# A gated-delta block: from the second block on, diagonal blocks of 32 are inverted on VectorE and one stage is left to TensorE

## The reference

```python
lower = jnp.where(strict, beta[..., :, None] * kk * decay, 0.0)
eye = jnp.eye(CHUNK, dtype=jnp.float32)
rhs = jnp.concatenate([beta[..., None] * v, beta[..., None] * k * jnp.exp(gc)[..., None]], axis=-1)
a_mat = jnp.broadcast_to(eye, lower.shape) + lower
sol = lax.linalg.triangular_solve(a_mat, rhs, left_side=True, lower=True, unit_diagonal=True)
```

## Time and profile before

| what | value |
|---|---|
| median of three executions | 2792.9 us (2784.8 to 2797.9) |
| the profiled execution | 2790.5 us |
| its span, first to last instruction | 2788.7 us |
| TensorE busy | 2710.8 us, 97% |
| VectorE busy | 1507.9 us, 54% |
| GpSimd busy | 1652.9 us, 59% |
| ScalarE busy | 1057.0 us, 38% |

### The profile page before, as it was taken

One profiled execution on the slowest core, in us unless ns is written; L12 is line 12 of the kernel. 1 busy time (PEld: TensorE's weight loads), 2 busy tenths in 40 slices (PEclk: granted clock), 3 DMA queues, 4 the chain that ended last, 5 costly groups with the idle time before them and its releaser, 6 DMA issues.

```text
span 2788.7 us, 36083 instructions
## 1 busy us (share of the span) xinstructions
PE 2710.8 (97%) x13344; PEld 2265.9 (81%) x13344; DVE 1507.9 (54%) x2439; ACT 1057.0 (38%) x1831; POOL 1652.9 (59%) x1244
## 2 busy tenths in 40 slices
PE   5999999999999999999999999999999999999998
PEld 4778887888888888888888888888888888888886
DVE  5878666474748566654546456563544553322223
ACT  3533332353334424343334433343333333433332
POOL 3745453676556756575556756575555666665653
PEclk9999998999999999999999999999999999999999
DMA  7334334432333323322233323422222223222232
GB/s 276 119 121 144 121 140 137 146 129 95 110 110 129 106 75 122 129 86 89 81 122 101 112 77 102 147 87 87 88 87 84 87 87 136 98 98 95 95 129 83
DMA packets 98094, 311.56 MB, mean 112 GB/s; under 512 B 11520, under 2 KB 11520, under 8 KB 95872
## 3 DMA queue, kind: packets, MB, share of 16 engines
q1 hardware_dynamic: 67248, 246.85, 25.5%
q10 hardware_dynamic: 30672, 62.40, 6.7%
HBM read 285.09 MB, written 24.12 MB: 111 GB/s over the span
## 4 chain that ended last, share of the span: by engine, by line
PE 86%; DVE 8%; issue 2%; POOL 2%; DMA 1%; ACT 1%; ACTq 0%; SPq 0%; POOLq 0%; DVEq 0%
PE acc L506 24%; PE acc L508 24%; PE acc L507 24%; PE pm L541 6%; PE pm L546 2%; DVE mixing L1229 1%; POOL w L1678 1%; PE pm L667 1%; PE pm L637 1%; DMA mixing<-in_ada_w 1%; PE pm L642 1%; DVE x L1510 1%; DVE octs L1334 1%; PE pm L638 1%; PE pm L653 0%
## 5 line engine op out<-in xcount | busy, mean ns | idle before, releaser
L1678 POOL TENSOR_TENSOR w<-raw,w 128x512 fp32r<-128x512 f32 x832 | 1134.1, 1366 | 1000.3 <-ACT w L749 998.0
L749 ACT ACTIVATE w<-raw 128x512 fp32r<-128x512 f32 x832 | 520.6, 627 | 775.9 <-PE acc L508 723.3
L506 PE MATMUL acc<-mT,w 128*128 128x512 f32 x1536 | 623.8, 406 | 8.5 <-DVE mT L1572 3.2
L508 PE MATMUL acc<-mT,w 128*128 128x512 f32 x1536 | 602.9, 393 | 0.0
L507 PE MATMUL acc<-mT,w 128*128 128x512 f32 x1536 | 601.5, 392 | 0.0
L506 PE MATMUL acc<-hid,w 128*128 128x512 f32 x864 | 348.8, 404 | 4.3 <-DVE ffs L1470 3.5
L506 PEld LDWEIGHTS acc<-mT,w 128*128 128x128 f32 x1536 | 291.4, 190 | 67.9 <-issue 5.1
L508 PEld LDWEIGHTS acc<-mT,w 128*128 128x128 f32 x1536 | 290.3, 189 | 63.4
L508 PE MATMUL acc<-hid,w 128*128 128x512 f32 x864 | 337.4, 390 | 0.0
L507 PE MATMUL acc<-hid,w 128*128 128x512 f32 x864 | 336.8, 390 | 0.0
L507 PEld LDWEIGHTS acc<-mT,w 128*128 128x128 f32 x1536 | 291.6, 190 | 54.8 <-issue 1.0
(11 more groups left out here) (231 smaller groups left out, 3697.4 us busy)
## 6 DMA issues: line engine op xcount, KB each, us to landing
raw<-in_w_all SPq DMA_DIRECT2D x416, 512.0 KB, 3.5
ada_late<-in_ada_w SPq DMA_DIRECT2D x32, 512.0 KB, 5.1
xr<-in_xT ACTq DMA_DIRECT2D x48, 256.0 KB, 3.5
mixing<-in_ada_w SPq DMA_DIRECT2D x8, 1024.0 KB, 9.8
proj_kept<-ffs ACTq DMA_DIRECT2D x32, 256.0 KB, 2.1
out<-io ACTq DMA_DIRECT2D x32, 256.0 KB, 2.4
mixed_kept<-mixing ACTq DMA_DIRECT2D x28, 256.0 KB, 2.2
xr<-mixed_kept ACTq DMA_DIRECT2D x28, 256.0 KB, 2.7
```

The lines of the kernel that those rows point to most:

```text
L506: e.matmul(bank, whi, x[:, 0, :], start=first, stop=False)
L508: m = e.matmul(bank, wlo, x[:, 0, :], start=False, stop=last)
L749: e.activation(w2[:, 0, local % HALVES, :], raw[:, tile % NRAW, local % 2 * NT:(local % 2 + 1) * NT], ACT.Copy).then_inc(S["w_hi"], 1)
L1678: e.tensor_tensor(w2[:, 1, local % HALVES, :], raw[:, tile % NRAW, local % 2 * NT:(local % 2 + 1) * NT], w2[:, 0, local % HALVES, :].bitca ...
```

## The change

From unit 4 on (`wide(n)`), VectorE inverts diagonal blocks of 32 rather than 8, in 31 steps of multiply, shuffle and add, two steps in each of the slots 19 to 34; TensorE's stage 0 and what belongs to it on the other engines is left out, and stage 1 keeps its slots. The mask of `Lm` moves from VectorE to GpSimd for all units. `attn` moves from slot 18 to 27, the two SiLUs from 21 to 26 and 28, `states` and `orr` one slot later, and the gates for the next block three slots later. Semaphore counts follow. One more mask of 128x128 is loaded at the start, and unit 4 makes two small constants.

```diff
@@ -590,8 +635,8 @@
-                if s in (16, 19, 23, 27):
-                    t = (16, 19, 23, 27).index(s)
+                if s in (16, 20, 24, 28):
+                    t = (s - 16) // 4
...
-                if 0 <= st < STAGES and step == 0:
-                    e.wait_ge(S["lvl_mask"], STAGES * n + st + 1)
-                    if st == 0:
+                if first_stage(n) <= st < STAGES and step == 0:
+                    e.wait_ge(S["lvl_mask"], stage_at(n, st) + 1)
+                    if st == first_stage(n):
...
                     e.wait_ge(S["proj_evac"], UNIT * m + RK + 1)
                     e.wait_ge(S["rot_q"], m)
                     e.wait_ge(S["r_upd"], m)
+                    if m and wide(m - 1):
+                        e.wait_ge(S["oct_steps"], oct_done(m))
...
+                if s == 18 and wide(n):
...
+                    e.wait_ge(S["oct_masked"], n + 1)
+                    e.tensor_reduce(wide_cols(near32), by_wide(Lm).rearrange("p t b j -> p t j b"), AX.X, ALU.add).then_inc(
+                        S["oct_steps"], 1)
+                    e.wait_ge(S["eye32_ready"], 2)
+                    e.wait_ge(S["r_upd"], n + 1)
+                    e.wait_ge(S["oct_steps"], oct_done(n) + 1)
+                    e.stream_shuffle(row32[0], near32, [0] * WIDE).then_inc(S["oct_steps"], 1)
+                for i in (range(2 * (s - 19), min(2 * (s - 19) + 2, WIDE - 1)) if wide(n) and 19 <= s < 35 else ()):
+                    done, low = oct_done(n) + 2 + 3 * i, i + 1 if i else 0
+                    row = wide_cols(row32[i % 2])
+                    before = wide_cols(inv32) if i else eye32.unsqueeze(1).to_broadcast([P, SUB, WIDE])
+                    e.wait_ge(S["oct_steps"], done)
+                    e.tensor_tensor(wide_cols(part32)[:, :, low:], row[:, :, low:],
+                                    before[:, :, i:i + 1].to_broadcast([P, SUB, WIDE - low]), ALU.mult).then_inc(S["oct_steps"], 1)
+                    if i + 1 < WIDE - 1:
+                        e.stream_shuffle(row32[(i + 1) % 2], near32, [i + 1] * WIDE).then_inc(S["oct_steps"], 1)
+                    e.wait_ge(S["oct_steps"], done + 1)
+                    e.tensor_tensor(wide_cols(inv32)[:, :, low:], before[:, :, low:], wide_cols(part32)[:, :, low:],
+                                    ALU.add).then_inc(S["oct_steps"], 1)
+                if s == 35 and wide(n):
+                    e.wait_ge(S["oct_steps"], oct_done(n + 1))
...
+                if s == 27:
+                    e.tensor_tensor(attn, bF, Dm, ALU.mult).then_inc(S["attn_ready"], 1)
...
+                if s == 17:
+                    e.wait_ge(S["lt_ready"], n + 1)
+                    near_mask = lmask32[:, :] if wide(n) else lmask[:, 0, :]
+                    e.tensor_tensor(by_sub(Lm), by_sub(LT), over_subs(near_mask), ALU.mult).then_inc(S["oct_masked"], 1)
+                if s in ((34,) if wide(n) else (26, 34)):
```

More of the change, by code:

```diff
@@ L36, with wide, oct_done, first_stage @@
 OCT = 8
+WIDE = 32
 OSTEPS = 1 + 3 * (OCT - 1)
+WSTEPS = 1 + 3 * (WIDE - 1)
+def wide(n):
+    return n >= HEADS
+def oct_done(n):
+    return OSTEPS * min(n, HEADS) + WSTEPS * max(n - HEADS, 0)
+def first_stage(n):
+    return 1 if wide(n) else 0
+def stage_count(n):
+    return STAGES * min(n, HEADS) + (STAGES - 1) * max(n - HEADS, 0)
+def stage_at(n, st):
+    return stage_count(n) + st - first_stage(n)
 SLOTS = 64
@@ L70, in dense_plan @@
                 e = kept[4 * n:4 * n + 4]
-                new = p[0:2] + e[0:1] + p[2:5] + e[1:2] + p[5:6] + e[2:3] + p[6:7] + e[3:4] + p[7:8]
+                if n:
+                    new = p[0:2] + e[0:1] + p[2:5] + e[1:2] + p[5:6] + e[2:3] + p[6:7] + e[3:4] + p[7:8]
+                else:
+                    new = p[0:4] + e[0:1] + p[4:6] + e[1:2] + p[6:7] + e[2:3] + p[7:8] + e[3:4]
             else:
@@ L342, in near_row, with wide_cols, by_wide @@
             return oct_cols(3 + i)
+        def wide_cols(ap):
+            return ap.rearrange("p (t j) -> p t j", j=WIDE)
+        near32, inv32 = (octs[:, 4 * i:4 * i + 4, :].rearrange("p a c -> p (a c)") for i in range(2))
+        row32 = [swp[:, i * P:(i + 1) * P] for i in range(2)]
+        part32 = swp[:, 2 * P:3 * P]
+        eye32 = octs[:, 8, :]
+        same32 = small[:, 48:52]
+        def by_wide(ap):
+            return ap.rearrange("p (t b j) -> p t b j", t=SUB, j=WIDE)
         def by_oct(ap):
@@ L608, in mix @@
                     else:
-                        e.wait_ge(S["t_next"], (STAGES - 1) * n + st)
+                        e.wait_ge(S["t_next"], n + 1)
                     four(bE, Lm, T).then_inc(S["x_out"], 1)
[L611 to L614, removed]
+                if first_stage(n) <= st < STAGES and step == 2:
+                    e.wait_ge(S["x_ready"], stage_at(n, st) + 1)
+                    if st > first_stage(n):
+                        e.wait_ge(S["u_turned"], n + 1)
                     else:
@@ L1321, in mix @@
                                            in1=sub(bA, t), op0=ALU.mult, op1=ALU.add).then_inc(S["r_state"], 1)
-                if s == 18:
-                    e.tensor_tensor(attn, bF, Dm, ALU.mult).then_inc(S["attn_ready"], 1)
-                    e.wait_ge(S["oct_steps"], OSTEPS * n + 1)
+                if s == 17:
+                    e.wait_ge(S["kk_out"], n + 1)
+                    e.wait_ge(S["beta_d"], n + 1)
+                    e.tensor_tensor(LT, bB, bD, ALU.mult).then_inc(S["lt_ready"], 1)
+                if s == 19 and not wide(n):
+                    e.wait_ge(S["oct_masked"], n + 1)
+                    e.tensor_reduce(near, by_oct(Lm).rearrange("p t b j -> p t j b"), AX.X, ALU.add).then_inc(S["oct_steps"], 1)
+                    e.wait_ge(S["oct_steps"], oct_done(n) + 1)
                     for i in range(OCT - 1):
-                        e.stream_shuffle(octs[:, 3 + i, :], octs[:, 0, :], [OCT * (q // OCT) + i for q in range(32)]).then_inc(S["oct_steps"], 1)
-                if 19 <= s < 19 + OCT - 1:
-                    i = s - 19
-                    done = OSTEPS * n + OCT + 2 * i
+                        e.stream_shuffle(octs[:, 3 + i, :], octs[:, 0, :], [OCT * (q // OCT) + i for q in range(32)]).then_inc(
+                            S["oct_steps"], 1)
+                for i in {20: (0, 1), 21: (2, 3), 22: (4, 5), 23: (6,)}.get(s, ()) if not wide(n) else ():
+                    done = oct_done(n) + OCT + 2 * i
                     if n == 0 and i == 0:
@@ L1337, in mix @@
                     e.tensor_tensor(inv8, before, part8, ALU.add).then_inc(S["oct_steps"], 1)
-                if s == 26:
-                    e.wait_ge(S["oct_steps"], OSTEPS * (n + 1))
+                if s == 25 and not wide(n):
+                    e.wait_ge(S["oct_steps"], oct_done(n + 1))
                     e.tensor_tensor(by_oct(U), inv8.unsqueeze(2).to_broadcast([P, SUB, P // OCT, OCT]),
```

135 lines of the change are left out of this document (71 added, 64 removed).

## The result

The changed kernel takes 2861.6 us, the median of four executions (2861.2 to 2871.6), beside 2790.6 for the kernel before: a ratio of 1.0268, 95% interval 1.0244 to 1.0292. It is 2.7% slower. The forecast was 2846 with a range of 2767 to 2900 and 0.68 for slower.

A forecast was written before the change was run, and what follows sets the result against it. TensorE, busy 97% of the span, was taken to bound the kernel. From the profiled 2790.5 us, 38.9 us of dropped calls were subtracted and 94 us of standing for VectorE added: 2846 us, range 2767 to 2900.

The forecast's parts named there:

- The gain: TensorE drops 48 stage-0 calls in 12 units at 0.81 us each, 38.9 us, counted in full.
- The step: One multiply, shuffle and add on VectorE takes 0.60 us undisturbed; 31 steps take 18.6 us a unit.
- The hold: GpSimd operations hold VectorE's multiplies and adds: 0.8 us for each of 198 in the windows, 158 us.
- VectorE's need: VectorE needs 414 + 158 = 572 us in the twelve windows, which TensorE would pass in 448.
- Standing and clock: TensorE stands 124 - 30 = 94 us in the windows for late VectorE; the sum had no clock term.
- The room: VectorE may be late by 2.5 us a unit, 30 us in all, before TensorE stands.
- The place: New idle time before dense matmuls, released by VectorE's evictions, slots 19 to 35, most in units 5 and 6, least in 11.
- TensorE's busy time: Sign of being right: in the new profile TensorE is busy about 39 us less.
- The moved slots: Moving orr, the SiLUs, attn and gates to other slots costs nothing; 12 us if dense products don't cover them.
- VectorE hides it: Rival, chance 0.12: GpSimd operations and steps seldom meet in the windows, TensorE never stands, 2751.6 us.
- GpSimd gives way: Rival, chance 0.20: GpSimd waits in dense VectorE runs, 0.5 us a meeting gives 2787 us, 0.4 gives 2767.
- Lateness drags the others: Rival, chance 0.16: ScalarE and GpSimd fall behind with VectorE, as if each hold cost 1.05 us, 2895 us.

The follow-up runs named there:

- kernel 2: Changed kernel with 7 of the 31 steps in a wide unit, one a slot, inverse left incomplete: 2757.3 us, ratio 0.9875 to the kernel before.
- kernel 3: Changed kernel with each multiply and add of the 31 steps replaced by a shuffle of the same size, inverse not computed: 2786.4 us, ratio 0.9976.
- Kernel 9: kernel 2 plus 14 reductions of 128x512 on VectorE ahead of slot 30's addition of squares in units 4, 8 and 12: 2791.3 us, ratio 0.9999.
- Kernel 4: Changed kernel with 16 of the 31 steps, one in each of slots 19 to 34, inverse left incomplete: 2787.6 us, ratio 0.9989.
- Kernel 5: Changed kernel with the MLP norm's column sums and what follows them two slots later in units 4, 8 and 12: 2861.4 us, ratio 1.0247.
- kernel 1: Changed kernel with no wide unit, only the moved slots and the mask of Lm on GpSimd left: 2792.9 us, ratio 1.0000.
- kernel 8: Changed kernel, all twelve units wide, multiply and add fused into one instruction per part, narrower shuffle, MLP norm two slots later: 2932.3 us, ratio 1.0501.

## Why the prediction was right

The direction, the mechanism and nearly the size were right: 2861.3 us in the profiled execution against 2845.6. Step by step:

- **The gain.** Forecast 38.9 us; kernel 2 gives 38.9 in its span and 34 between medians. The exact match of the spans is chance: TensorE's busy time is 49.0 us less there, of which the clock gives some 10, and its idle time 10.1 us more (88.0 against 77.9).
- **The step.** Forecast 0.60 us in the mean; 0.71 at 116 elements and 0.50 at 16 to 24 fit it. The medians of 233 and 226 ns lie in the forecast's 0.20 to 0.25; the maxima, 1.37 and 1.40 us, a little over its 1.3.
- **The hold.** The mechanism is shown by kernel 3, the price was too high: 0.8 us for each GpSimd operation. After has 215 of them in the windows, and VectorE's busy time without holds is 110.5 us lower, 0.51 us for each. Only 131 of the 744 multiplies and adds lasted over 0.5 us; their mean is 1.16, that of the others 0.22, and so the holds counted one by one are 123 us, 0.57 for each GpSimd operation. "Each GpSimd operation has one held operation beside it" holds for 6 in 10. The rule of the Trainium skill ("SBUF — State Buffer", "Who interferes with whom") is right for one pair, as the add of 2029.40 shows again, but taken for every GpSimd operation (2943 us) it counts meetings that don't happen.
- **VectorE's need.** Forecast 572 us, windows measured 587.6, although holds cost 35 to 48 us less. VectorE is busy for 90% of them, not over 95%. The other 57 us it waits: in units 4, 8, 11 and 12 8.0 to 8.5 us each, and 6.3 us of the 57 for GpSimd's mask, by the groups of lines:

```profile
L1396 DVE TENSOR_REDUCE octs<-mixing 128x128 f32<-128x512 f32 x12 | 13.4, 1114 | 6.3 <-POOL mixing L1816 6.3
```

  Two errors of opposite sign met here; the near hit of 572 is in part luck.
- **Standing and clock.** Forecast 94 us of idle time; measured 159.4 - 77.9 = 81.5 more, 68 of them in the windows. But a price was missing, that of TensorE's clock behind a pause. Span by span, 2859.4 - 2788.7 = 70.7 = -38.9 + 81.5 + 28, so 28 us are left beside idle time. The clock has most of them: laid over TensorE's busy time, its records give 84.7 us of work at the low level in after and 41.7 before, and half of the 43.0 between, 21.5 us, is lost. The other 6.5 us no row assigns. The mean clock would say 32 us (1 - 0.980 of the one span is 57, 1 - 0.991 of the other 25), since it counts the low level during the waits too. All together, 109.6 us, stands against the forecast's 94. Kernel 9 shows the coupling by itself: beside kernel 2 it has 20.4 us more of work at the low level, and TensorE's busy time is 10.0 us longer. The Trainium skill says in "TensorE: Matmul & The Clock Gate", "Part 1: The HAM clock gate (the "warmup" mystery)", that the throttled level is the default and that activity releases it; the rows at 587.87 agree. By it a term for the clock was due beside the term for standing.
- **The room.** The windows are 587.6 - 448.2 = 139.4 us too long. TensorE lost 109.6 us over the whole span, so 30 were hidden, as in the forecast. In the mean 2.5 us a unit was good, for the single unit it was not: unit 13's window is 45.5 us where TensorE needs 38.8 - 2.4 = 36.4, 9.1 too long. Its idle time (45.50 - 42.75) and its clock (0.96) cost 2.8 + 1.8 us, so 4.5 were hidden. Kernel 4's table shows the other side, units with next to none.
- **The place.** Wrong in part. The forecast had the evictions of dense products release the waits. They do for 22.3 + 11.6 us. The largest group, 25.7 of 29.1 us, is the column sums of the MLP's norm in units 4, 8 and 12, and one of 10.1 us is the turn of `orr`. TensorE's idle time in its windows is largest in unit 6 (10.4 us) and least in 11 (2.4), as forecast, but units 4, 8, 12 and 15 come next, with 8.4 to 8.8, ahead of 5. Kernel 5 shows that the place is not the cause.
- **TensorE's busy time** is 10.8 us less and not 39: a matmul at the low clock counts 0.63 instead of 0.39 us. In kernel 2, at a clock of 0.994, it is 49.0 us less.
- **The moved slots** cost nothing (kernel 1).

The sum: with gain and room as forecast, the 15.6 us by which the windows were longer are the 15.7 us by which the forecast was low. That the total comes so near is in part luck. The holds were put 35 to 48 us too high and the idle time 12.5, and against them stand two terms that the sum did not have, VectorE's own waits (57 us) and TensorE's clock (21.5).

Of the rivals, "VectorE hides it" falls by kernel 4: even 16 steps cost 30 us. "GpSimd gives way" has its price of 0.5 us a meeting confirmed, but not its time, since VectorE's own waits and the clock took the place of the holds; and GpSimd's median, 1293 ns by the trace, is what it was (1295), so it hardly gave way. "Lateness drags the others" began but did not reach TensorE: ScalarE waits 83.4 us for the squares of FF1, before 49.3, but TensorE's wait for GpSimd's part of the weights (line 1754) is 1.9 us, before 2.9.

What stays open: how idle time and clock would divide if evictions alone were late, and what VectorE's idle time in units 4, 8 and 12 would be without the low clock beside it. No run isolates either. Nor does one take the clock away by itself.

## What to carry to other kernels

Work moved from a full engine to one with free time must fit that engine's free time in each stretch, with what it costs there in company, and not its share of the span: VectorE was at 54% overall, and 31 small dependent steps in a unit still took more than they gave. Ask of each small VectorE operation with two inputs in SBUF which GpSimd operations it will meet, and measure it by swapping in an operation of the same length that can't be held. An engine that starts to wait in long pieces is also slower behind them, so a forecast of idle time on TensorE needs a second term for the clock.

## What the runs showed of the hardware

- A wait of TensorE of 8.4 to 9.0 us is followed by 7.0 us at the lower clock level (kernels after and 9 alike), dense starts 0.43 instead of 0.23 us apart. The low level also came behind shorter ones: after waits of 0.37 and 1.82 us in unit 13 seven dense matmuls of after ran at it, the fifth to the eleventh behind the second wait. That these waits are the cause was not tested. TensorE's timeline:

```profile
2046.54 0.47 PE L551 MATMUL acc<-hid,w 128*128 128x512 f32 x1 [0.37 <-DVE x L1556]
...
2051.37 0.47 PE L551 MATMUL acc<-hid,w 128*128 128x512 f32 x1 [1.82 <-DVE x L1556]
2051.67 0.40 PE L552 MATMUL acc<-hid,w 128*128 128x512 f32 x1
...
2052.43 0.63 PE L552 MATMUL acc<-hid,w 128*128 128x512 f32 x1
2052.86 0.63 PE L553 MATMUL acc<-hid,w 128*128 128x512 f32 x1
...
2055.78 0.39 PE L551 MATMUL acc<-hT,w 128*128 128x512 f32 x1
```

- Multiply by a column and add in one instruction, 26 elements, costs 0.16 us from start to start (four from 564.95 to 565.58 in kernel 8), where a plain multiply of 36 elements costs 0.12 (585.50 to the shuffle at 585.62, in the timeline of after). Fused, a step of 104 elements took 0.80 us and not 0.68: it had five instructions in place of three.
